# A one-layer hybrid trunk with routed experts: LayerNorm between the row sums on VectorE, the SSM and convolution tails on GpSimd in whole buffers, another table order on ScalarE, another order of work ahead of the first expert

## The chip, the cores and the metric

The kernel runs on one core of one Trainium2 chip. Its time is the device time of one execution in microseconds (us), and the figure compared is the median of several runs. The text uses the profile's names for the engines: PE is TensorE, DVE is VectorE, ACT is ScalarE, POOL is GpSimd, SP is SyncE, whose queue issues most of the DMAs. Each engine runs its own list of instructions in order and waits on semaphores for the others.

## The reference

The input is x, 1024 tokens by 1024 features, float32, one layer. Cut to what matters here:

```python
h = rms_norm(x, mix_norm)
c_q, c_kv, k_pe, u_ssm, conv_a, conv_g = split(h @ w_in)
y_attn = mla_mixer(...)     # 8 heads; q, k RMS-normed per head, rotary on 32 of 96 dims, block-causal softmax
y_ssm  = s5_mixer(...)      # z = gelu(y); out = z * sigmoid(z @ w_glu)        width 256
y_conv = conv_mixer(...)    # silu(layer_norm(conv31(a * sigmoid(g)) + b))     width 256
x = x + concat(rms_norm(y_attn), rms_norm(y_ssm), rms_norm(y_conv)) * out_norm @ w_out
h = rms_norm(x, ffn_norm)
# router: first the best of 4 groups, then the best 2 of its 8 experts, with gates
x = x + sum(gate_e * (silu(h @ w1[e]) * (h @ w3[e])) @ w2[e])   # 32 experts, d_ff 512, float32
```

## The kernel before

**Stages.** The 1024 tokens are 8 tiles of 128 (NT = 8). After the input projection, the convolution (on DVE, to 182 us) and the SSM scan, the kernel projects q, k and v tile by tile (`save_qkv` on ACT). Then come three things that this change touches: a stretch in which LayerNorm, the q/k norms and the SSM tail are made (about 206 to 262 us), the attention loop (262 to 459 us), and the stretch from the last output tile to the first expert (576 to 640 us). Behind it a loop over 34 blocks of 128 rows (32 experts and two overflow blocks) runs to the end at 1262 us.

**Norms and LayerNorm.** POOL squares the q and k of tile i (`square_qk`, L593) into two buffers that alternate, so it may be at most two tiles ahead of DVE, which sums them (`sum_qk`, L1360). POOL squares tiles 0 and 1, then waits for DVE's statistics (`ln_stats`), makes 1/sqrt of the variance (L606 and L607, `ln_rstd`), and squares tiles 2 to 7. DVE sums tiles 0 and 1, makes LayerNorm's statistics (L1371, L1374), waits for `ln_rstd`, normalizes (L1379), applies weight and bias in two operations over the whole buffer `ctok` (L1383, L1384), then sums tiles 2 to 7 (L1391). The sum of squares of all heads goes to ACT for its square root (L870), and DVE refines it. Then DVE makes head 0's q and k (`make_heads_part`, L353) and signals `head0_made`. POOL makes heads 1 to 7, and starts head 1 on `qk_scaled` (L611), which comes ahead of DVE's head 0. Two heads' buffers alternate.

**ACT's order there:** Silu of `ctok` (L854), Gelu of the SSM output in two halves (L862, signal `z_ready`), the square root (L870), the copy of the transposed z (`zT`, L873), Sigmoid (L878) behind PE's 32 matmuls with w_glu (L1894), the two copies of head 0's k (`save_kT`, L935). A change of function needs an ACT_TABLE_LOAD.

**Attention loop.** A step n is one head and one tile of queries; STEPS is 64, 8 steps a head, with the tiles in the order 7, 6, 1, 0, 5, 4, 3, 2. PE makes the scores two steps ahead, DVE takes the row maximum (L1440), ACT the exponentials (L945), PE transposes them (L1964), ACT and DVE copy them out, PE multiplies by the values once in two steps (L1976). Beside it the next head's q and k are transposed in four parts through one PSUM bank (`turn_head`, steps 1 to 4 of each head, L1912), and in heads 0 to 3 ACT does one piece of the y tail at the end of each step (`y_step`, L899):

```python
CONV_SQUARE_AT, SSM_SQUARE_AT, CONV_SCALE_AT, SSM_SCALE_AT = (range(NT * h, NT * (h + 1)) for h in range(4))
Y_TURN_AT = {NT * (3 + k // 4) + 5 + k % 4: k for k in range(NT)}
```

A square is an ACTIVATE with an accumulator, a scale another ACTIVATE (L883, L888). The product of Sigmoid and z is one DVE operation at step 3 (`gate_ssm`, L1415). POOL makes both 1/rms behind head 4 (L626 to L630). In heads 3 and 4 PE transposes y (`turn_y`) and ACT copies it. The loads of w_out wait for the last copy (L426). In heads 6 and 7 ACT and DVE split w_out and y in two parts (`high_y_piece`, `rest_y_piece`).

**Into the experts.** In the second output projection the SP queue stores each tile of h2 (the normed rows, which experts gather from) and of x2 (into `out`). Ahead of the last tile's two stores it issues three loads of 2 MB, w1 of expert 0 and w1 and w3 of expert 1 (L447 to L454); w3 of expert 0 was loaded long before. ACT waits for all stores of x2 (`out_stored`, L1049), since the rounded copy of w3 lies where x2 was, and only then makes the rounded copies of w1 and w3 (`high_w13`), four operations. POOL waits for the h2 stores and the routing table (L650, L651), copies an index for the scatter (`prepare`) and gathers expert 0's and 1's rows (L653). DVE makes the rests of w1, of the gathered rows, and of w3 (L1675 to L1677), then the overflow table (L1679 to L1704), whose signal `ov_table` lets SP issue the loads of w2 of experts 0 and 1 (L461 to L466). From then on SP issues each load when PE has used up the buffer: `next_up`, `next_down`.

Of the kernel before, what the change touches and what calls it, by code (L numbers as in the profile page):

```python
# [22 lines left out]
P = 128  # L23
# [13 lines left out]
def build(nc, x, positions, mix_norm, w_in, q_a_norm, w_uq, kv_a_norm, w_ukv, q_norm, k_norm,  # L37
# [34 lines left out]
    with ExitStack() as ctx:  # L72
# [69 lines left out]
        sout = at(S0 + 12640, NT, SW)  # L142
        cperm = at(S0 + 14592, 2, NT, P)
# [133 lines left out]
        ln_done, z_ready, glu_done, mid_squared = sems("ln_done z_ready glu_done mid_squared")  # L277
# [27 lines left out]
        conv_done, qk_mean, qk_root, qk_scaled, head0_made, heads_made, y_half_filled = sems("conv_done qk_mean qk_root qk_scaled head0_made heads_made y_half_filled")  # L305
# [33 lines left out]
        CONV_SQUARE_AT, SSM_SQUARE_AT, CONV_SCALE_AT, SSM_SCALE_AT = (range(NT * h, NT * (h + 1)) for h in range(4))  # L339
        Y_TURN_AT = {NT * (3 + k // 4) + 5 + k % 4: k for k in range(NT)}  # L340
# [33 lines left out]
        def _(sp):  # L374
# [148 lines left out]
        def _(pool):  # L523
# [78 lines left out]
            for i in range(2):  # L602
# [5 lines left out]
            for i in range(2, NT):  # L608
                square_qk(i)

            pool.wait_ge(qk_scaled, 1)  # L611
# [7 lines left out]
            for h in range(1, H):  # L619
# [108 lines left out]
        def _(act):  # L728
# [136 lines left out]
            link(last)  # L865
            act.sem_inc(z_ready, 1)
            act.sem_inc(hi_drained, 1)

            act.wait_ge(qk_mean, 1)
            act.activation(at(14336 + 2816, 2 * NT * H), qks.rearrange("p a i h -> p (a i h)"), ACT.Sqrt).then_inc(qk_root, 1)  # L870
# [1334 lines left out]
```

## Time and profile before

| | |
|---|---|
| Median of 3 runs | 1266.5 us (1263.73 to 1268.53) |
| The profiled execution | 1263.85 us, span 1262.1 us |
| PE busy | 1131.8 us (90%) |
| DVE busy | 980.6 us (78%) |
| ACT busy | 712.6 us (56%) |
| POOL busy | 376.2 us (30%) |
| DMA | 260.93 MB, mean 207 GB/s |
| Mean granted PE clock | 0.963 of full |

The span runs from the first to the last instruction of the profiled execution; 1.75 us of its time lie outside. Busy shares are averages over stages with different limits, so what counts is which wait ends last in a stretch.

### The profile page before, as it was taken

The page shows a single profiled execution, that of the slowest core. Times are in us where ns is not written, and L with a number is a line of the kernel's source. Part 1 is how long each engine was busy: PE and PEld are TensorE (multiplying, and loading weights), DVE is VectorE, ACT ScalarE, POOL GpSimd, SP SyncE. Part 2 cuts the span into 40 slices and gives each one's busy share as a digit, 9 for nine tenths or more (in the row PEclk, how much of TensorE's full clock was granted, in tenths as well). Part 3 has the DMA queues.
Part 4 walks back from the last instruction along what each step waited for, and adds up shares of the span by engine and source line. Part 5 has one row for each costly group of instructions (what it writes and reads, how often), then busy time and mean ns, then how long its engine had stood idle before and what let it go on. Part 6 is the DMA issues. An engine that isn't in the chain of part 4 may idle for free.

```text
span 1262.1 us, 15972 instructions
## 1 busy us (share of the span) xinstructions
PE 1131.8 (90%) x5636; PEld 866.9 (69%) x5636; DVE 980.6 (78%) x1179; ACT 712.6 (56%) x865; POOL 376.2 (30%) x354
## 2 busy tenths in 40 slices
PE   5899999769899889996699999999999999999992
PEld 3447565546566568785578888888877877787781
DVE  1969998865555746366699999998988998898871
ACT  5521226455555652221577777777777777777751
POOL 2304005565534000011223233333333333334221
PEclk9899989899999999997799999999999999999996
DMA  6600000000004010337399999999999999999940
GB/s 202 163 0 1 0 12 16 2 0 2 1 1 194 41 34 1 122 128 274 115 425 384 368 396 379 394 397 376 388 372 373 372 354 373 369 350 372 359 149 10
DMA packets 55484, 260.93 MB, mean 207 GB/s; under 512 B 31088, under 2 KB 31760, under 8 KB 41616
## 3 DMA queue, kind: packets, MB, share of 16 engines
q1 hardware_dynamic: 45344, 243.03, 49.8%
q0 software_dynamic: 10096, 17.34, 5.7%
q8 instruction: 26, 0.43, 0.1%
q14 instruction: 18, 0.15, 0.0%
HBM read 252.25 MB, written 26.35 MB: 221 GB/s over the span
## 4 chain that ended last, share of the span: by engine, by line
PE 56%; DVE 19%; DMA 12%; issue 4%; ACT 3%; SPq 2%; POOL 2%; DVEq 0%; POOLq 0%; ACTq 0%
PE psum L2116 25%; DMA w<-in_w 10%; PE psum L2136 10%; PE psum L2028 7%; DVE arena L1312 5%; DVE arena L1114 4%; PE psum L1976 3%; PE psum L1946 2%; PE psum L1762 2%; PE psum L1964 2%; DMA out<-arena 2%; PE psum L2106 1%; DVE am L1440 1%; PE psum L2122 1%; PE psum L1932 1%
## 5 line engine op out<-in xcount | busy, mean ns | idle before, releaser
L1652 DVE TENSOR_TENSOR w_rest<-w,w_high 128x2048 fp32r<-128x2048 f32 x136 | 305.1, 2285 | 20.2 <-ACT w_high L1036 19.7
L1036 ACT ACTIVATE w_high<-w 128x2048 fp32r<-128x2048 f32 x136 | 256.4, 1912 | 93.7 <-DMA w<-in_w 62.6
L2116 PE MATMUL psum<-w_high,xgT_high 128*128 128x512 f32 x544 | 217.8, 400 | 15.2 <-DVE xgT_rest L1645 15.1
L2116 PE MATMUL psum<-w_rest,xgT_high 128*128 128x512 f32 x544 | 213.5, 393 | 0.0
L2116 PE MATMUL psum<-w_high,xgT_rest 128*128 128x512 f32 x544 | 213.4, 392 | 0.0
L1659 DVE TENSOR_TENSOR w_rest<-w,w_high 128x2048 fp32r<-128x2048 f32 x68 | 152.4, 2282 | 1.8 <-ACT w_high L1046 1.8
L1046 ACT ACTIVATE w_high<-w 128x2048 fp32r<-128x2048 f32 x68 | 126.4, 1908 | 26.2 <-DMA w<-in_w 26.2
L2116 PEld LDWEIGHTS psum<-w_high,xgT_high 128*128 128x128 f32 x544 | 102.9, 189 | 41.3 <-issue 16.8
L671 POOL DMA_INDIRECT out<-arena,idx x34 | 91.6, 2694 | 107.5 <-DVE arena L1672 102.2
L2116 PEld LDWEIGHTS psum<-w_rest,xgT_high 128*128 128x128 f32 x544 | 103.0, 189 | 22.0
L2116 PEld LDWEIGHTS psum<-w_high,xgT_rest 128*128 128x128 f32 x544 | 103.1, 190 | 20.1
L2136 PE MATMUL psum<-w_high,heT_high 128*128 128x512 f32 x272 | 109.5, 402 | 7.3 <-DVE heT_rest L1640 7.3
L2136 PE MATMUL psum<-w_high,heT_rest 128*128 128x512 f32 x272 | 106.6, 392 | 0.0
L2136 PE MATMUL psum<-w_rest,heT_high 128*128 128x512 f32 x272 | 106.4, 391 | 0.0
L1762 PE MATMUL psum<-arena 128*128 128x512 f32 x224 | 99.5, 606 | 3.0 <-ACT arena L743 3.0
L655 POOL COPY idx<-arena 128x2 int32 (+1 forms) x34 | 36.3, 1068 | 178.0 <-PE psum L2106 163.2
L538 POOL TENSOR_SCALAR st<-st 128x1 f32<-128x1 f32 (+1 forms) x21 | 7.1, 338 | 275.9 <-ACTq L996 96.8
L664 POOL COPY idx<-arena 128x2 int32 (+1 forms) x35 | 40.4, 1156 | 143.0 <-DMA out<-arena,idx 112.2
L1762 PEld LDWEIGHTS psum<-arena 128*128 128x128 f32 x224 | 43.4, 195 | 57.4 <-issue 57.4
L945 ACT ACTIVATE arena<-psum,am 128x1024 f32<-128x1024 f32 (+3 forms) x64 | 47.4, 741 | 58.6 <-DVE am L1440 55.8
L1946 PE MATMUL psum<-arena 96*128 96x512 f32 (+1 forms) x192 | 73.6, 493 | 0.8 <-DVE arena L1431 0.8
L1312 DVE SCALAR_TENSOR_TENSOR arena<-arena,dwc 128x1024 f32<-128x1024 f32 x58 | 69.4, 1272 | 0.0
(268 smaller groups left out, 2034.9 us busy)
## 6 DMA issues: line engine op xcount, KB each, us to landing
w<-in_w SPq DMA_DIRECT2D x102, 2048.0 KB, 19.5
arena<-in_x SPq DMA_DIRECT2D x5, 1024.0 KB, 4.9
h_scratch<-arena SPq DMA_DIRECT2D x8, 512.0 KB, 2.6
out<-arena SPq DMA_DIRECT2D x8, 512.0 KB, 3.6
arena<-in_x SPq DMA_DIRECT2D x1, 3072.0 KB, 20.6
arena<-in_w_in SPq DMA_DIRECT2D x1, 2688.0 KB, 14.8
arena<-in_w_in SPq DMA_DIRECT2D x1, 2048.0 KB, 12.1
wout_y_raw<-in_w_out SPq DMA_DIRECT2D x1, 2048.0 KB, 9.2
```

Source lines behind the costliest of these rows:

```text
L671: pool.indirect_dma_start(out=out_d, out_offset=bass.IndirectOffsetOnAxis(ap=idx[:, 2 + b, 0:1], axis=0), in_=ye[b], in_offset=None, bound ...
L1036: act.activation(w13h[k][:, c, :], w13[b][k][:, c, :], ACT.Copy).then_inc(W13H_READY[k], 1)
L1046: act.activation(w2h[:, c, :], w2s[b][:, c, :], ACT.Copy).then_inc(w2h_ready, 1)
L1114: link(dve.tensor_tensor(out_, a, b_, op))
L1312: ins = dve.scalar_tensor_tensor(cacc[:, m, :], src, dwc[:, m, k:k + 1], cacc[:, m, :], M_, A_)
L1652: dve.tensor_tensor(w13l[b][k][:, c, :], w13[b][k][:, c, :], w13h[k][:, c, :].bitcast(F32), S_).then_inc(W13_SPLIT[k], 1)
L1659: dve.tensor_tensor(w2l[b][:, c, :], w2s[b][:, c, :], w2h[:, c, :].bitcast(F32), S_).then_inc(w2_split, 1)
L1762: last = pe.matmul(bank, win[:, c, c0:c0 + P], hT[:, c, 4 * half:4 * half + 4, :].rearrange("p i j -> p (i j)"), start=(c == 0), stop=(c = ...
L1946: last = pe.matmul(psum[:, 2 * (n % 2) + k, 0:w], qT[h % 2][0:QH, i * P:(i + 1) * P], kT[h % 2][0:QH, 512 * k:512 * k + w], start=True, st ...
L2028: last = pe.matmul(psum[:, 2 * (i % 2) + k, :], x_[:, c, i * P:(i + 1) * P], w_[:, c, 512 * k:512 * (k + 1)], start=(c == 0 and n == 0), s ...
L2116: last = pe.matmul(psum[:, k, :], x_[:, c, :], w_[:, c, :], start=(c == 0 and n == 0), stop=(c == KC - 1 and n == 2))
L2136: last = pe.matmul(psum[:, 5 + k, :], h_[:, c, :], w_[:, c, 512 * k:512 * (k + 1)], start=(c == 0 and n == 0), stop=(c == FC - 1 and n == 2))
```

## The change

It has five parts. (1) POOL squares four tiles ahead of `ln_rstd`, and DVE sums tiles 2 and 3 while POOL makes `ln_rstd`, 4 and 5 behind the normalization, 6 between LayerNorm's two operations and 7 behind them. POOL's head 1 waits for `head0_made`. (2) ACT takes the square root between the two Gelu halves, and Silu of `ctok` behind them. (3) The y tail leaves ACT: POOL squares and scales `ctok` and `sout` and makes the product in operations over the whole 128 x 2048 buffer; DVE sums the squares in four operations at steps 7, 9, 25 and 27. (4) The transposes of the next head move to steps 2 to 5, those of y one step later. (5) Ahead of the first expert, the last x2 and h2 tiles are stored behind one weight load and ahead of the other two; ACT rounds w1 before it waits for `out_stored`; DVE makes half of w1's rest ahead of the table and w3's ahead of the rows'; POOL gathers before it copies the scatter's index.

```diff
+        y_squares = at(S0 + 18784, NT, SW)
...
+        Y_SUM_AT = {NT - 1: 0, NT + 1: 1, 3 * NT + 1: 2, 3 * NT + 3: 3}
+        Y_TURN_AT = {NT * (3 + k // 4) + 6 + k % 4: k for k in range(NT)}
         def next_part(n):
-            return (n // NT + 1, n % NT - 1) if n // NT + 1 < H and 1 <= n % NT <= 4 else None
+            return (n // NT + 1, n % NT - 2) if n // NT + 1 < H and 2 <= n % NT <= 5 else None
...
                 if i == NT - 1:
                     sp.wait_ge(out_filled, NT)
                     sp.dma_start(w13[0][0], w1_e[0]).then_inc(W13_IN[0][0], 16)
-                    sp.dma_start(w13[1][0], w1_e[1]).then_inc(W13_IN[1][0], 16)
-                    sp.dma_start(w13[1][1], w3_e[1]).then_inc(W13_IN[1][1], 16)
+                    sp.wait_ge(x2_ready, NT)
+                    sp.dma_start(out_s[:, i, :], x2[:, i, :]).then_inc(out_stored, 16)
                 sp.wait_ge(h2_ready, i + 1)
                 sp.dma_start(h2_s[:, i, :], h2[i % 2]).then_inc(H2_OUT[i % 2], 16)
-                sp.dma_start(out_s[:, i, :], x2[:, i, :]).then_inc(out_stored, 16)
+                if i < NT - 1:
+                    sp.dma_start(out_s[:, i, :], x2[:, i, :]).then_inc(out_stored, 16)
+            sp.dma_start(w13[1][0], w1_e[1]).then_inc(W13_IN[1][0], 16)
+            sp.dma_start(w13[1][1], w3_e[1]).then_inc(W13_IN[1][1], 16)
...
-            for i in range(2):
+            for i in range(4):
                 square_qk(i)
             pool.wait_ge(ln_stats, 1)
...
+            def square_y(src):
+                pool.tensor_tensor(y_squares, src, src, ALU.mult).then_inc(mid_squared, 1)
+            def scale_y(src, col, second):
+                pool.wait_ge(mid_summed, 2 * second + 2)
+                rms(col, col + 8, CW, NT, EPS, mid_rms)
+                pool.wait_ge(mid_rms, second + 1)
+                pool.tensor_tensor(src, src, st[:, col + 8:col + 8 + NT].unsqueeze(2).to_broadcast([P, NT, CW]),
+                                   ALU.mult).then_inc(mid_scaled, 1)
-            pool.wait_ge(qk_scaled, 1)
+            pool.wait_ge(head0_made, 1)
...
-                if h == 4:
-                    pool.wait_ge(mid_squared, 1)
-                    rms(64, 72, CW, NT, EPS, mid_rms)
-                    pool.wait_ge(mid_squared, 2)
-                    rms(48, 56, SW, NT, EPS, mid_rms)
+                if h == 1:
+                    pool.wait_ge(conv_act_done, 1)
+                    square_y(ctok)
+                if h == 2:
+                    scale_y(ctok, 64, 0)
+                if h == 3:
+                    pool.wait_ge(hi_drained, R_GLU + 1)
+                    link(pool.tensor_tensor(sout, sout, yssm, ALU.mult))
+                    square_y(sout)
+                if h == 5:
+                    scale_y(sout, 48, 1)
...
-            prepare(0, 0)
             gather(0, 0)
             gather(1, 1)
+            prepare(0, 0)
...
-            act.wait_ge(ln_done, 1)
-            link(act.activation(ctok, ctok, ACT.Silu))
...
+            save_z(0)
+            act.wait_ge(qk_mean, 1)
+            act.activation(at(14336 + 2816, 2 * NT * H), qks.rearrange("p a i h -> p (a i h)"), ACT.Sqrt).then_inc(qk_root, 1)
+            link(save_z(1))
             act.sem_inc(z_ready, 1)
             act.sem_inc(hi_drained, 1)
+            act.wait_ge(ln_done, 1)
+            act.activation(ctok, ctok, ACT.Silu).then_inc(conv_act_done, 1)
             act.wait_ge(hi_filled, R_Z + 1)
...
-                y_step(n)
+                if n in Y_TURN_AT:
+                    save_y_turned(Y_TURN_AT[n])
...
-            act.wait_ge(out_stored, 16 * NT)
             act.wait_ge(out_filled, NT)
             act.sem_inc(y_saved_a, 1)
-            for k in range(2):
-                for h in range(2):
-                    high_w13(k, 0, 0, h, W13_IN[0][k], 16)
+            for h in range(2):
+                high_w13(0, 0, 0, h, W13_IN[0][0], 16)
+            act.wait_ge(out_stored, 16 * NT)
+            for h in range(2):
+                high_w13(1, 0, 0, h, W13_IN[0][1], 16)
...
             dve.sem_inc(ln_stats, 1)
+            for i in range(2, 4):
+                sum_qk(i)
             dve.wait_ge(ln_rstd, 1)
             for i in range(NT):
                 last = dve.tensor_scalar(ctok[:, i, :], pc[i], bns[:, i, 6:7], st[:, 112 + i:113 + i], S_, M_)
             link(last)
             dve.sem_inc(hi_drained, 1)
+            for i in range(4, 6):
+                sum_qk(i)
...
             tt(ctok, ctok, lnwb[:, 0, :].unsqueeze(1).to_broadcast([P, NT, CW]), M_)
+            sum_qk(6)
             tt(ctok, ctok, lnwb[:, 1, :].unsqueeze(1).to_broadcast([P, NT, CW]), A_)
             dve.sem_inc(ln_done, 1)
+            sum_qk(7)
...
-                tt(sout, sout, yssm, M_)
+            def sum_y(k):
+                col, i0 = (64, 48)[k // 2], 4 * (k % 2)
+                dve.wait_ge(mid_squared, k // 2 + 1)
+                dve.reduce_sum(st[:, col + i0:col + i0 + 4], y_squares[:, i0:i0 + 4, :], AX).then_inc(mid_summed, 1)
...
+            rest_w13(0, 0, 0, (0,))
             dve.wait_ge(tab_filled, 2)
             save_table(0, NE, 1)
             dve.sem_inc(tab_ready, 1)
...
             dve.sem_inc(y_saved_v, 1)
-            rest_w13(0, 0, 0)
+            rest_w13(0, 0, 0, (1,))
+            rest_w13(1, 0, 0)
             rest_xgT(0)
-            rest_w13(1, 0, 0)
```

## Rows read from the trace of the kernel before

**Rows 1.** Stretches, heads 0 to 5: length, busy PE, PEld, DVE, ACT, POOL; clock, DMA, GB/s.

```profile
270.91:371.03 100.12, 86.61 (x626) 60.02 (x628) 57.03 (x169) 59.56 (x156) 53.08 (x61) 0.97 0.00 1
371.03:394.92 23.89, 22.23 (x170) 15.79 (x172) 13.69 (x42) 13.00 (x31) 13.13 (x18) 1.00 0.00 1
394.92:416.38 21.46, 20.20 (x155) 13.97 (x155) 13.54 (x42) 10.64 (x25) 1.23 (x4) 1.00 0.86 343
```

**Rows 2.** The timeline of DVE from 206 us: start, us; idle before, and what ended it.

```profile
216.05 3.71 DVE L1379 TENSOR_SCALAR arena<-psum,bns,st 128x256 f32<-128x256 f32 x8 [2.11 <-POOL st L607]
...
219.91 5.44 DVE L1114 TENSOR_TENSOR arena<-arena,lnwb 128x2048 f32<-128x2048 f32 x2
...
231.03 0.95 DVE L1362 TENSOR_REDUCE qks<-arena 128x8 f32<-128x768 f32 x1 [0.88 <-POOL arena L600]
...
278.18 2.28 DVE L1114 TENSOR_TENSOR arena<-arena 128x2048 f32<-128x2048 f32 x1
```

**Rows 3.** The timeline of ACT, the same stretch.

```profile
226.70 1.91 ACT L854 ACTIVATE arena<-arena 128x2048 f32<-128x2048 f32 x1
...
229.93 1.47 ACT L862 ACTIVATE arena<-psum 128x128 f32<-128x128 f32 x8
...
233.68 1.28 ACT L870 ACT_TABLE_LOAD   x1 [0.17 <-ACT arena L862]
...
240.81 0.31 ACT L870 ACTIVATE arena<-qks 128x128 f32<-128x128 f32 x1 [5.84 <-DVEq L1398]
...
252.52 2.06 ACT L878 ACTIVATE arena<-psum 128x512 f32<-128x512 f32 x4 [8.16 <-PE psum L1894]
...
259.27 0.59 ACT L935 ACTIVATE arena<-psum 96x512 f32<-96x512 f32 x1 [4.68 <-PE psum L1932]
```

**Rows 4.** The timeline of PE, the same stretch.

```profile
243.12 9.37 PE L1894 MATMUL psum<-arena 128*128 128x256 f32 x32 [7.41 <-ACT arena L873]
...
258.14 3.44 PE L1932 MATMUL psum<-ident,arena 128*96 128x128 f32 x16 [5.66 <-DVEq L1411]
...
262.37 3.49 PE L1946 MATMUL psum<-arena 96*128 96x512 f32 x8 [0.78 <-DVE arena L1431]
```

**Rows 5.** The timeline of POOL, from 206 us.

```profile
230.95 1.47 POOL L599 TENSOR_TENSOR arena<-arena 128x768 f32<-128x768 f32 x1
...
243.58 2.21 POOL L361 TENSOR_TENSOR arena<-arena,qks 128x768 f32<-128x768 f32 x1 [5.31 <-DVEq L1407]
...
319.36 1.65 POOL L540 TENSOR_TENSOR st<-st,minus_half 128x8 f32<-128x8 f32 x1
```

**Rows 6.** The waits of head 1 (296.81 to 322.17): us in total, times, longest.

```profile
ACT arena L888 <- POOL st L540: 2.5, 1, 2.5
```

**Rows 7.** The chain of waits ahead of the first expert, its longest piece.

```profile
583.73 19.28 DMA out<-arena
```

**Rows 8.** The timeline of all engines ahead of the first expert.

```profile
598.99 0.19 DVE L1117 TENSOR_SCALAR arena<-psum 128x32 int32<-128x32 f32 x1 [3.14 <-PE psum L2073]
...
601.94 0.19 POOL L664 COPY idx<-arena 128x2 int32<-128x2 int32 x1 [20.45 <-DMA h_scratch<-arena]
...
603.14 7.31 ACT L1036 ACTIVATE w_high<-w 128x2048 fp32r<-128x2048 f32 x4 [16.05 <-DMA out<-arena]
...
606.70 1.94 PE L2106 MATMUL psum<-ident,arena 128*128 128x128 f32 x8 [7.83 <-DMA arena<-h_scratch,idx]
...
612.54 4.48 DVE L1652 TENSOR_TENSOR w_rest<-w,w_high 128x2048 fp32r<-128x2048 f32 x2
...
612.67 0.80 PE L2116 MATMUL psum<-w_high,xgT_high 128*128 128x512 f32 x1 [4.03 <-DVE xgT_rest L1645]
```

**Rows 9.** The timeline of the SP queue: the first load after the gap.

```profile
623.66 0.34 SPq L465 DMA_DIRECT2D w<-in_w  x1
```

**Rows 10.** DMA issues, windows 650:700, then 900:950: count, KB, us to landing.

```profile
w<-in_w SPq DMA_DIRECT2D x9, 2048.0 KB, 11.1
...
w<-in_w SPq DMA_DIRECT2D x9, 2048.0 KB, 21.4
```

More of the change, by code:

```diff
@@ L607, in _ @@
             pool.tensor_tensor(st[:, 112:112 + NT], st[:, 112:112 + NT], minus_half[:, 0:NT], ALU.pow).then_inc(ln_rstd, 1)
-            for i in range(2, NT):
+            for i in range(4, NT):
                 square_qk(i)
-            pool.wait_ge(qk_scaled, 1)
+            def square_y(src):
[7 more added lines that the diff above has]
+            pool.wait_ge(head0_made, 1)
             n = [0]
@@ L864, in _ @@
                                               ACT.Gelu_apprx_tanh)
-            link(last)
+                return last
+            save_z(0)
+            act.wait_ge(qk_mean, 1)
+            act.activation(at(14336 + 2816, 2 * NT * H), qks.rearrange("p a i h -> p (a i h)"), ACT.Sqrt).then_inc(qk_root, 1)
+            link(save_z(1))
             act.sem_inc(z_ready, 1)
             act.sem_inc(hi_drained, 1)
-            act.wait_ge(qk_mean, 1)
-            act.activation(at(14336 + 2816, 2 * NT * H), qks.rearrange("p a i h -> p (a i h)"), ACT.Sqrt).then_inc(qk_root, 1)
+            act.wait_ge(ln_done, 1)
+            act.activation(ctok, ctok, ACT.Silu).then_inc(conv_act_done, 1)
             act.wait_ge(hi_filled, R_Z + 1)
@@ L880, in _ @@
             act.sem_inc(hi_drained, 1)
-            def square_y(src, i, col):
-                link(act.activation(tmp[:, 0:CW], src[:, i, :], ACT.Square, accum_out=st[:, col + i:col + 1 + i]))
-                if i == NT - 1:
-                    act.sem_inc(mid_squared, 1)
-            def scale_y(src, i, col):
-                link(act.activation(src[:, i, :], src[:, i, :], ACT.Copy, scale=st[:, col + i:col + 1 + i]))
-                if i == NT - 1:
-                    act.sem_inc(mid_scaled, 1)
             def save_y_turned(k):
@@ L1364, in sum_qk @@
                 dve.sem_inc(qk_summed, 1)
-            sum_qk(0)
-            sum_qk(1)
+            kp2 = at(14336 + 2560, NT, RD)
+            for i in range(2):
+                sum_qk(i)
             dve.wait_ge(hi_filled, R_CONV + 1)
@@ L1381, in _ @@
             dve.sem_inc(hi_drained, 1)
+            for i in range(4, 6):
+                sum_qk(i)
+            dve.wait_ge(scratch_in, 16)
+            tt(kp2, kpe, kpe, M_)
+            link(dve.reduce_sum(st[:, 120:120 + NT], kp2, AX))
             dve.wait_ge(row_par_in, 16 * 8)
+            ts(qkw[:, 0, :], qkw[:, 0, :], SCALE, None, M_)
             tt(ctok, ctok, lnwb[:, 0, :].unsqueeze(1).to_broadcast([P, NT, CW]), M_)
+            sum_qk(6)
             tt(ctok, ctok, lnwb[:, 1, :].unsqueeze(1).to_broadcast([P, NT, CW]), A_)
             dve.sem_inc(ln_done, 1)
-            dve.wait_ge(scratch_in, 16)
-            kp2 = at(14336 + 2560, NT, RD)
-            tt(kp2, kpe, kpe, M_)
-            link(dve.reduce_sum(st[:, 120:120 + NT], kp2, AX))
-            ts(qkw[:, 0, :], qkw[:, 0, :], SCALE, None, M_)
-            for i in range(2, NT):
-                sum_qk(i)
+            sum_qk(7)
             tt(qks[:, 1], qks[:, 1], st[:, 120:120 + NT].unsqueeze(2).to_broadcast([P, NT, H]), A_)
@@ L1405, in _ @@
             tt(qk_f, qk_f, qkr, M_)
-            dve.sem_inc(qk_scaled, 1)
             for a in range(2):
@@ L1481, in _ @@
                         save_qT(h, part // 2)
+                if n in Y_SUM_AT:
+                    sum_y(Y_SUM_AT[n])
                 if n % 2 == 1:
                     save_ohT(n // 2)
-                if n == 3:
-                    gate_ssm()
                 if n - 1 in Y_PIECE_AT:
@@ L1601, in _, with rest_w13 @@
             ts(tokf[:, :], toki[:, :], -SKIP_ROW, None, A_)
+            def rest_w13(k, b, e, halves=(0, 1)):
+                for h in halves:
+                    c = slice(h * KC // 2, (h + 1) * KC // 2)
+                    dve.wait_ge(W13H_READY[k], 2 * e + (h + 1))
+                    dve.tensor_tensor(w13l[b][k][:, c, :], w13[b][k][:, c, :], w13h[k][:, c, :].bitcast(F32),
+                                      S_).then_inc(W13_SPLIT[k], 1)
             def normalize(i):
@@ L1646, in rest_xgT @@
                                   xgTh.rearrange("p c n -> p (c n)").bitcast(F32), S_).then_inc(xgT_saved, 1)
-            def rest_w13(k, b, e):
-                for h in range(2):
-                    c = slice(h * KC // 2, (h + 1) * KC // 2)
-                    dve.wait_ge(W13H_READY[k], 2 * e + (h + 1))
-                    dve.tensor_tensor(w13l[b][k][:, c, :], w13[b][k][:, c, :], w13h[k][:, c, :].bitcast(F32),
-                                      S_).then_inc(W13_SPLIT[k], 1)
             def rest_w2(b, e):
```

29 lines of the change are left out of this document (3 added, 26 removed).

## The prediction

> **What bounds the kernel now.** The stretches first [rows 1]. In heads 0 to 5 of the attention loop PE is busy 87% to 94% of every stretch and DVE at most 63%, but the lengths differ though PE's and DVE's work hardly do: heads 0 to 3 take 100.12 us together, 25.0 each, head 4 takes 23.89, head 5 takes 21.46. ACT goes with them, 59.6 us busy in the four, 14.9 a head, and 10.64 in head 5, which has none of the y tail. The steps are chains that go PE, DVE, ACT, PE; a piece of ACT work between two links lengthens them. Then the timelines of the four engines from 206 to 262 us [rows 2 to 5]: DVE bounds it, with its waits for POOL (2.11 us, later 0.88) and its waits for nobody; PE starts the first scores at 262.37. Then the waits of head 1 [rows 6]: ACT sat 2.5 us for POOL's 1/rms, because POOL makes it behind head 4. Last the stretch ahead of the experts: the chain of waits has a piece of 19.28 us that is one store [rows 7], since it queues behind 6 MB of weights; behind it ACT starts its roundings at 603.14, POOL its gather, PE its first expert matmul at 612.67 [rows 8]. The SP queue issues the next load at 623.66 [rows 9]. In the expert loop the weights' time to landing grows from 11.1 to 21.4 us [rows 10] while PE uses them at a steady pace: the stream is the slower of the two, and its start counts as much as PE's.
>
> **Part 1 and 2, LayerNorm and ACT's order.** DVE's idle for `ln_rstd` (2.11 us) is filled with two sums that it needs anyway, and so are four waits for POOL's squares (0.88 in the row; three more like it of 0.75, so 3.1): POOL is now two tiles ahead each time. That is 5.2 us. Against it, one of LayerNorm's two multiplies now starts beside POOL's last square. Before, the two took 5.44 us with POOL running for the first 0.96 us, against 2.28 for one alone [rows 2]: that overlap cost 0.9. Now about 2 us overlap, so I charge 0.9 to 1.4 more, and take 1.2. ACT's root, at 240.81 before [rows 3], comes at 236.8, 4.0 earlier.
>
> The SBUF page of the Trainium skill (SBUF — State Buffer, Who interferes with whom) says that a DVE operation with two SBUF inputs and a POOL operation that reads SBUF exclude each other for whole instructions. By that rule the charge would be the rest of one POOL square, 0.4 us, and the sum 0.8 better; the 0.9 us above for an overlap of 0.96 agrees with it.
>
> From the root on the new chain is ACT's. Root 0.31, table load 1.28, second Gelu half 1.47, hand-over 0.2; PE turns z under the next table load (1.28) and Silu (1.91); then the four copies of zT, priced as the Sigmoid's four of the same size, 2.06 [rows 3]. That is 8.5 us: PE's w_glu matmuls start at 245.3 instead of 243.12, and take 9.37 again [rows 4], to 254.7. Then Sigmoid 2.06 with 0.2 to hand over, and two copies of k of 0.59 each: first scores at 258.2 instead of 262.37, **4.1 us** earlier. Head 0 is not on this path any more. DVE came from the root at 240.81 to head 0's end at 258.1, where PE's turn starts [rows 4]: 17.3 us, with POOL's head 1 beside it from 243.58 on [rows 5]. Even unchanged these end at 254.1, ahead of 254.7; DVE's 2048 columns in 2.28 us give about 7 us for head 0 without POOL beside it, an end near 247. POOL's head 1, put behind it, takes some 13 us, to 260 or at the worst 267, and is first needed in step 2 of head 0, about 268. **Bounds:** if PE's matmuls run wholly at the high clock they are 2 us shorter; if the squares do not keep up, 2 of the 4.1 go.
>
> **Part 3, the y tail.** Off ACT go 8 operations per head in heads 0 to 3, off DVE the product of 2.28 us in head 0 [rows 2], which sat in the chain. On DVE come four sums of 1024 columns; 768 take 0.95 [rows 2], so 1.3 each. Those at steps 9 and 25 lie in DVE's wait for PE's longest multiply; those at 7 and 27 cost between 0 and 1.3, I take 0.7. So head 0 becomes 21.46 + 0.9 = 22.3, head 1 with half of the one at the border 21.8, head 2 21.5 (its 2.5 us wait for POOL [rows 6] gone with the rest), head 3, which has the four turns of y as head 4 has, 23.89 + 0.5 = 24.4: 90.0 instead of 100.12 [rows 1]. With 0.5 us in the first steps this is **10.6 us**. The bounds are 5 (the heads keep 23, since some other link takes the place) and 14.
>
> POOL gets, behind heads 1, 2, 3 and 5, five operations over 2048 columns. 768 columns take it 1.47 [rows 5], so 3.9 at most, and two 1/rms of 1.65 + 0.2. Beside them it needs some 13 a head (13.13 in head 4 [rows 1]), so it has room; the tight place is `turn_head(3, 0)`, step 18. The second sum comes in step 9, about 291.5; 1/rms 1.9, scale 3.9, head 3 13.1: 310.4. PE wants it at about 315, 2.1 heads behind the first scores. Slack 4.6 us.
>
> **Part 4, the later turns.** It costs nothing of itself; the parts move from the step with the longest value multiply to short ones. I take 0, between -3 and +3 over seven heads. The turns of y end a step later, so w_out's 4 MB start some 2.7 us later against step 49: at the 343 GB/s of the row of head 5 [rows 1] they need 12.3 us of the 21.5 that remain. Hidden.
>
> **Part 5, into the first expert.** The last stores queue behind 2 MB and no more: at 6 MB in about 19 us, they land some 12 us earlier, about 590. POOL's wait (601.94 before) ends with the routing table instead (DVE starts to write it at 598.99, so 599.5), and the index copy comes first: it gains 2.4, and gives back about 1.0, since DVE's rests now run beside its two copies and its gather (an operation of 768 columns takes POOL 2.21 beside DVE and 1.47 alone [rows 5]); the bounds of that are 0 and all 2.4. So rows land about 1.4 earlier, at 605.3 instead of 606.7. Then turn 1.94, ACT's copy 1.0 at once (ACT's 7.31 us of roundings [rows 8] ran to 610.46 before and now end by 596), the rest 1.24: PE starts at 609.7 instead of 612.67, **3.0 us** earlier. DVE made w3's rest (4.48 us) behind the rows' before [rows 8]; now ahead. So the overflow table starts 7 us earlier, and with it the loads at 623.66 [rows 9]. That load stream is then 4 us further ahead of PE; by the growing landing times [rows 10] PE gets nearly all of it back later as stalls that do not come. I take **6.5 us** for the end, between 3.0 (PE's own start) and 7.5.
>
> **The sum.** 4.1 + 10.6 + 6.5 = 21.2 us. Against the profiled execution's 1263.85 this is 1242.65. The median of the runs shown lies 2.65 above it, so the forecast is **1245.3 us**.
>
> **Rivals.** (a) *The heads are bound by another link.* For it: PE is busy 87% in heads 0 to 3, and in head 5 POOL was nearly idle (1.23 us), so 21.46 may be a price without POOL. Against: DVE's busy time is the same in both kinds of head. The loop would give 5 or less, 1251. Chance 0.13. (b) *The stream is paced by PE after all*, the early loads only fill buffers sooner: the end gives 3.0, and if the gather loses all to DVE 1, 1249 to 1251. For it: landing in 11.1 us still leaves PE unstalled. Chance 0.10. (c) *POOL comes late, and it ends slower.* POOL runs in order, and head 3 sits behind a sum, 1/rms and a scale, head 4 behind a product and a square. Under DVE's two-input work POOL's operations can take twice as long. At double price, 7.9 us each, head 3 comes within its slack and head 4 about 3 us late: 1248. It needs 13 us per operation to eat the 21 us; at 15.7, head 3 is 7 late and head 4 19 late, 1271. Nothing in the loop has DVE read twice from SBUF, so chance 0.02. The GPSIMD page of the Trainium skill (GPSIMD Engine Reference, Elementwise — side-by-side cycle accounting) gives 4.5 us for such an operation and would leave elementwise work on DVE; by that price the slack at head 3 is 4.0 instead of 4.6, and the sum the same. (d) *The parts cancel*, as the ACT chain of part 2 loses what part 1 gains and the heads give little: 1260 to 1266. Chance 0.03.
>
> **How the numbers follow.** The forecast has 0.72. Its own bounds, 2 us on either side in part 1, 5 and 14 for the loop, 3 and 7.5 for the end, do not all fall together: 1239 to 1251. Taking in (a) and (b) needs 1254 at the top. 0.5%, about what a measurement of this kernel can tell from no change, is 6.3 us: faster than 1260.2 holds the forecast, (a) and (b), 0.95; I leave 0.93, within 0.04, slower 0.03.
>
> **What would show it.** Right: ACT's Sigmoid starts near 254.7 and the first scores near 258; no ACT square or scale in the loop, heads 0 to 2 each under 22.5 us; POOL's head 3 done before PE asks for it; the last x2 store lands near 590, PE's first expert matmul some 3 us closer to the last output tile, SP's next load some 7 us closer. Wrong: a wait of PE for POOL in heads 2 or 3, heads above 23 us with ACT idle, or an expert loop as long as before from PE's first matmul to the end.

## The result, and the profile after

The changed kernel takes **1254.6 us** (median of five executions; 1253.5 to 1258.1) where the one before takes 1266.5 (also five): ratio 0.992, interval 0.990 to 0.994. A second measurement of the same file gave 1256.1 against 1266.0, ratio 0.991 (0.989 to 0.993). The gain is 10 to 12 us, about half of the 21.2 forecast. The profiled execution took 1256.61 us, its span 1254.5.

The stretches of heads 0 to 3, head 4 and head 5 after, with the columns of [rows 1]:

```profile
267.06:362.83 95.77, 83.66 (x624) 57.81 (x625) 60.05 (x173) 45.87 (x109) 72.40 (x71) 1.00 0.00 1
362.83:388.20 25.37, 22.27 (x170) 15.79 (x169) 13.87 (x42) 13.06 (x32) 12.58 (x15) 1.00 0.00 1
388.20:411.20 23.00, 20.41 (x154) 14.01 (x153) 13.69 (x42) 11.28 (x27) 2.88 (x9) 1.00 0.80 320
```

Heads 0 to 3 take 4.35 us less than in [rows 1], where 10.1 was forecast, and heads 4 and 5, in which the y tail never had a square or scale, are 1.5 us each **longer** though PE and DVE are busy within 0.25 us of what they were. Something new stands in every head. The waits of head 5 name it (engine and line, who is waited for, us in total, times, longest):

```profile
ACT arena L936 <- DVE am L1435: 6.9, 4, 2.7
...
PE psum L1928 <- ACT arena L926: 1.8, 2, 1.1
```

L1928 is PE's transpose of the next head's q and k (`turn_head`), L926 is ACT's copy of the turned k (`save_kT`), L936 the exponentials and L1435 DVE's row maximum. In head 5 before, PE had no wait for that copy. The timeline of all engines, after, shows the first of the two:

```profile
392.00 0.60 PE L1928 MATMUL psum<-ident,arena 128*96 128x128 f32 x4
...
392.39 0.96 DVE L1435 TENSOR_REDUCE am<-psum 128x1 f32<-128x768 f32 x1
...
392.55 1.25 PE L1942 MATMUL psum<-arena 96*128 96x512 f32 x4
...
393.38 0.90 ACT L936 ACTIVATE arena<-psum,am 128x768 f32<-128x768 f32 x1 [2.44 <-DVE am L1435]
...
394.27 0.58 ACT L926 ACTIVATE arena<-psum 96x512 f32<-96x512 f32 x1
...
394.91 0.64 PE L1928 MATMUL psum<-ident,arena 128*96 128x128 f32 x4 [1.12 <-ACT arena L926]
```

The four transposes of part 0 end at 392.60. ACT could copy them at once, but its list has the exponentials of step n+2 first, and it sits 2.44 us waiting for their row maximum. So the copy runs at 394.27, and PE, which has one bank for these turns, starts part 1 at 394.91, 1.12 us after it was ready. Part 3 loses 0.64 in the same way.

Ahead of the loop, in the timelines that answer to [rows 2] to [rows 5]:

```profile
225.30 0.98 DVE L1107 TENSOR_TENSOR arena<-arena 128x256 f32<-128x256 f32 x1
...
225.96 1.65 POOL L603 TENSOR_TENSOR arena<-arena 128x768 f32<-128x768 f32 x1
...
226.77 0.90 DVE L1110 TENSOR_SCALAR qkw<-qkw 128x96 f32<-128x96 f32 x1
227.57 1.03 POOL L604 TENSOR_TENSOR arena<-arena 128x512 f32<-128x512 f32 x1
227.71 3.05 DVE L1107 TENSOR_TENSOR arena<-arena,lnwb 128x2048 f32<-128x2048 f32 x1
...
237.57 0.31 ACT L887 ACTIVATE arena<-qks 128x128 f32<-128x128 f32 x1 [5.16 <-DVEq L1394]
...
240.91 3.60 PE L1846 MATMUL psum<-ident,arena 128*128 128x128 f32 x16 [8.69 <-ACTq L890]
...
244.55 2.06 ACT L895 ACTIVATE arena<-psum 128x512 f32<-128x512 f32 x4 [0.52 <-PE psum L1846]
...
246.67 8.86 PE L1890 MATMUL psum<-arena 128*128 128x256 f32 x32 [2.15 <-ACT arena L895]
...
255.57 2.06 ACT L900 ACTIVATE arena<-psum 128x512 f32<-128x512 f32 x4 [7.65 <-PE psum L1890]
...
258.98 3.46 PE L1942 MATMUL psum<-arena 96*128 96x512 f32 x8 [1.70 <-ACT arena L926]
```

The first scores start at 258.98 instead of 262.37. Ahead of the first expert, in the timeline of all engines, and the two rows of DMA issues (windows 650:700 and 900:950) are:

```profile
595.39 0.19 DVE L1110 TENSOR_SCALAR arena<-psum 128x32 int32<-128x32 f32 x1 [0.73 <-PE psum L2069]
...
597.19 2.25 POOL L678 DMA_INDIRECT arena<-h_scratch,idx  x1 [0.96 <-POOL idx L675]
...
603.76 1.02 ACT L1000 ACTIVATE xgT_high<-psum 128x1024 fp32r<-128x1024 f32 x1 [9.76 <-PE psum L2102]
...
606.10 0.29 PEld L2112 LDWEIGHTS psum<-w_high,xgT_high 128*128 128x128 f32 x1 [2.77 <-DVE xgT_rest L1648]
...
612.69 0.34 SPq L469 DMA_DIRECT2D w<-in_w  x1
```

```profile
w<-in_w SPq DMA_DIRECT2D x9, 2048.0 KB, 8.7
...
w<-in_w SPq DMA_DIRECT2D x8, 2048.0 KB, 20.3
```

POOL now gathers 1.8 us behind the table, and has waited for no store. ACT's four roundings ran from 586.69 to 594.00 without a pause, so the last store of x2 had landed by 590.4, as forecast. From the table's first write to PE's first expert matmul it is 10.71 us (595.39 to 606.10) instead of 13.68 (598.99 to 612.67). The next load comes 6.59 us behind that matmul instead of 10.99. But from PE's first expert matmul to the end it takes 648.4 us where it took 649.4.

### The profile page after: what moved, and what is told of

It is laid out like the page before. It is cut to its first block, busy times and chain, and to the rows that moved or that the text cites. A ratio compares the mean times of both kernels' runs of the same rounds, so it can differ in the third digit from the quotient of the medians.

```text
span 1254.5 us, 15926 instructions
## 1 busy us (share of the span) xinstructions
PE 1130.0 (90%) x5636; PEld 866.9 (69%) x5636; DVE 978.3 (78%) x1182; ACT 700.2 (56%) x818; POOL 378.5 (30%) x359
## 4 chain that ended last, share of the span: by engine, by line
PE 60%; DVE 19%; DMA 9%; issue 4%; ACT 4%; SPq 2%; POOL 0%; DVEq 0%; ACTq 0%; POOLq 0%
PE psum L2112 26%; PE psum L2132 11%; DMA w<-in_w 9%; PE psum L2024 6%; DVE arena L1305 6%; DVE arena L1107 5%; PE psum L1972 3%; PE psum L1942 2%; PE psum L1758 2%; PE psum L1960 2%; PE psum L2102 2%; DVE am L1435 1%; PE psum L2118 1%; PE psum L1928 1%; DVE arena L1110 1%
## 5 line engine op out<-in xcount | busy, mean ns | idle before, releaser
L1038 ACT ACTIVATE w_high<-w 128x2048 fp32r<-128x2048 f32 x68 | 126.3, 1908 | 20.3 <-DMA w<-in_w 20.2
L675 POOL COPY idx<-arena 128x2 int32 (+1 forms) x34 | 27.5, 808 | 201.7 <-PE psum L2102 169.0
L936 ACT ACTIVATE arena<-psum,am 128x1024 f32<-128x1024 f32 (+3 forms) x64 | 47.3, 740 | 59.7 <-DVE am L1435 58.5
L684 POOL COPY idx<-arena 128x2 int32 (+1 forms) x35 | 33.2, 948 | 113.3 <-DMA out<-arena,idx 102.8
```

The lines of the kernel that those rows point to most:

```text
L1038: act.activation(w2h[:, c, :], w2s[b][:, c, :], ACT.Copy).then_inc(w2h_ready, 1)
```

## The experiments

Two theories stood after this. **T**: the later turns cost some 1.5 us a head through ACT's copy, and the rest of the forecast is about right. Its rival **S**: the heads are long for another reason, POOL's whole-buffer work above all, and the turns are innocent. For the experts, **A**: the lead of the weight stream counts, **B**: only PE's own start does. Each ratio is against the kernel before, measured beside it (medians 1265.8 to 1266.2).

**1. The changed kernel again.**

> The changed kernel itself, on the chip of the three runs beside it. Both theories: about 10 to 12 us below the kernel before (ratio 0.991 to 0.993), heads 0 to 5 of the attention loop at 23.5, 23.0, 23.0, 26.4, 25.4 and 22.9 us, as its first trace has them.

Measured: 1256.1 us, ratio 0.991 (0.989 to 0.993); first scores at 258.71, heads 23.55, 22.98, 22.98, 26.27, 25.37, 23.00. The result repeats.

**2. The turns back.**

```diff
-Y_TURN_AT = {NT * (3 + k // 4) + 6 + k % 4: k for k in range(NT)}
+Y_TURN_AT = {NT * (3 + k // 4) + 5 + k % 4: k for k in range(NT)}
-    return (n // NT + 1, n % NT - 2) if n // NT + 1 < H and 2 <= n % NT <= 5 else None
+    return (n // NT + 1, n % NT - 1) if n // NT + 1 < H and 1 <= n % NT <= 4 else None
```

> The changed kernel with the transposes of the next head back in steps 1 to 4 and those of y back by one step; all else of the change stays. Theory T (the later turns cost 1.5 us a head, because PE, one step later, waits for ACT's copies of k, which stand behind the exponentials): heads 0 to 2 and 5 fall to 21.5 or 22, PE's waits for L926 vanish from them, first expert matmul 9 to 11 us earlier than in the changed kernel, median 8 to 11 us below it, about 1245. Rival S (the heads are longer for another reason: POOL's whole-buffer operations, DVE's sums, or ACT without its y work running differently): the heads stay within 0.5 us of 23, the median within 3 us of the changed kernel.

Measured: **1244.3 us**, ratio 0.982 (0.980 to 0.984), 11.8 less than the changed kernel on the same chip, where 8 to 11 were expected. Its stretches of heads 0 to 3, 4 and 5:

```profile
267.31:356.82 89.51, 83.06 (x626) 57.78 (x625) 59.21 (x173) 45.95 (x110) 69.49 (x68) 1.00 0.00 1
356.82:380.71 23.89, 22.23 (x169) 15.79 (x169) 13.68 (x42) 12.99 (x32) 17.08 (x23) 1.00 0.00 1
380.71:402.20 21.49, 20.23 (x154) 14.00 (x153) 13.51 (x42) 10.69 (x26) 1.25 (x4) 1.00 0.85 343
```

Heads 4 and 5 are back at the 23.89 and 21.46 of [rows 1], with the whole y tail on POOL. The turns carry all of what was missing: over heads 0 to 6 this trace is 11.3 us shorter than that of the changed kernel.

**3. The turns late, alone**, in the kernel before: the reverse of the edit of 2.

> The kernel before with nothing but the turns moved to steps 2 to 5 (and those of y one step later). Theory T: PE waits 1 to 2 us a head for ACT's copies of k, more in heads 0 to 3 where ACT still has the y tail; the head with nothing beside it (head 5) goes from 21.46 to 22.9, the median 7 to 12 us above the kernel before. Rival S: within 3 us of the kernel before, head 5 at 21.5.

Measured: 1279.7 us, ratio 1.010 (1.008 to 1.012), 13.8 slower, more than the 7 to 12 expected; head 5 is 23.01. The cost needs nothing else of the change. PE's waits in the heads before the y tail is through (270.95 to 373) are:

```profile
PE psum L1932 <- ACT arena L935: 8.6, 8, 2.2
```

Here too PE's turn (L1932 in this file) waits for ACT's copy of k (L935), eight times in four heads. In head 5, which has no y tail beside it, two such waits take 1.8 us, as in the changed kernel.

**4. The copy first.** The turns stay late; ACT's list changes.

```diff
-                if n + 2 < STEPS:
-                    exponentials(n + 2)
                 if next_part(n):
                     h, part = next_part(n)
                     if part % 2 == 0:
                         save_kT(h, part // 2)
+                if n + 2 < STEPS:
+                    exponentials(n + 2)
```

> The changed kernel with ACT's copy of k put ahead of the exponentials of the same step instead of behind them; turns stay in steps 2 to 5. Theory T with this mechanism: the copy fits into the 2.4 us that ACT waits there for DVE's maximum, PE's waits of 1.1 and 0.6 us for it vanish, heads 0 to 2 and 5 at 21.5 to 22, median 6 to 10 us below the changed kernel. If only the place of the transposes on PE costs (its own work in the short steps) and not ACT's copy, the heads stay at 23 and the median within 3 us of the changed kernel. A loss is possible where the copy delays the exponentials: then ACT's waits for DVE shrink and PE's for the exponentials grow.

Measured: **1243.3 us**, ratio 0.983 (0.981 to 0.985), 12.8 below the changed kernel where 6 to 10 were expected. Its stretches of heads 0 to 3, 4 and 5, then the same place of head 5 in the timeline:

```profile
265.91:354.43 88.52, 82.69 (x625) 58.02 (x625) 59.28 (x173) 45.96 (x109) 68.97 (x67) 1.00 0.00 1
354.43:377.93 23.50, 22.08 (x170) 15.84 (x169) 13.67 (x42) 13.07 (x32) 16.10 (x19) 1.00 0.00 1
377.93:399.07 21.14, 20.23 (x154) 14.06 (x153) 13.49 (x42) 11.31 (x27) 2.92 (x9) 1.00 0.87 348
```

```profile
381.73 0.60 PE L1928 MATMUL psum<-ident,arena 128*96 128x128 f32 x4
...
382.12 0.96 DVE L1435 TENSOR_REDUCE am<-psum 128x1 f32<-128x768 f32 x1
...
382.37 0.59 ACT L926 ACTIVATE arena<-psum 96x512 f32<-96x512 f32 x1 [1.69 <-PE psum L1928]
383.12 0.90 ACT L936 ACTIVATE arena<-psum,am 128x768 f32<-128x768 f32 x1 [0.15 <-DVE am L1435]
383.36 0.60 PE L1928 MATMUL psum<-ident,arena 128*96 128x128 f32 x4
```

The copy fits into what was ACT's wait, the exponentials start 0.04 us behind the row maximum, and PE's second turn comes 1.63 us behind the first instead of 2.91. One swap of two calls takes the cost away with the turns where they were, so the late copy is the cause. The heads are even 0.35 us shorter than with the turns back (21.14 against 21.49).

**5. Both**, turns back and copy first.

> The changed kernel with the turns at steps 1 to 4 as before and ACT's copy of k ahead of the next exponentials. Theory: the cost is ACT's copy standing behind exponentials that wait for DVE's row maximum; with the copy first the place of the turns does not matter, so heads are 21.0 to 21.7 us and the median lies within 2 us of the copy-first version (1243.3). Rival: the place of the turns has a price of its own (they lengthen PE's longest step), then it is 2 to 5 us slower or faster than copy-first.

Measured: 1246.2 us, ratio 0.984 (0.982 to 0.986); heads 0 to 3 take 89.50 and head 5 21.49, as in 2. With the turns at steps 1 to 4 the place of the copy does not matter, since PE had no such wait there. The theory's second half, that with the copy first the place of the turns does not matter either, missed its 2 us: the later place is the better one, by 1.7 us over heads 0 to 5 in the two traces. The medians lie 2.9 apart, but were taken on two chips, and the intervals of their ratios overlap; so the size of this smaller effect is not settled.

**6. Parts 1 and 2 alone** (LayerNorm between the sums, ACT's order, POOL's head 1 behind head 0), on the kernel before.

```diff
             save_z(0)
+            act.wait_ge(qk_mean, 1)
+            act.activation(at(14336 + 2816, 2 * NT * H), qks.rearrange("p a i h -> p (a i h)"), ACT.Sqrt).then_inc(qk_root, 1)
             link(save_z(1))
...
-            pool.wait_ge(qk_scaled, 1)
+            pool.wait_ge(head0_made, 1)
```

> The kernel before with parts 1 and 2 alone: LayerNorm between the sums, POOL four tiles ahead, root between the Gelu halves, Silu behind them, POOL's head 1 behind head 0; the y tail, turns and part 5 as before. First scores at 258.5 to 259.5 instead of 262.4, heads as before. If these 3.4 us are kept to the end: 3 to 4 us faster, about 1262.5. Rival: POOL's head 1, made behind head 0, is late for the turns at step 1 of head 0, and head 0 grows by 1 to 3 us; then 0 to 2 us faster.

Measured: 1261.2 us, ratio 0.997 (0.995 to 0.999), 5.0 faster, where 3 to 4 were expected; first scores at 258.13. Head 0 takes 24.30 us, as it does in the trace of part 5 alone (24.29), which changes nothing ahead of it. The rival falls.

**7. Part 3 alone** (the y tail on POOL, DVE's four sums), on the kernel before.

```diff
+                if h == 1:
+                    pool.wait_ge(conv_act_done, 1)
+                    square_y(ctok)
...
-                y_step(n)
+                if n in Y_TURN_AT:
+                    save_y_turned(Y_TURN_AT[n])
```

> The kernel before with part 3 alone: the y tail on POOL in whole buffers, DVE's four sums, turns at steps 1 to 4 as before. The prediction's part 3: heads 0 to 2 under 22.5 us, head 3 at 24.4 to 24.6, heads 4 to 7 as before, 10.6 us faster in all. By difference from the other runs (21.7 with the turns back, less 5.0 for the norms and 5.5 for part 5) it should be 10 to 12 us faster than before, 1254 to 1256. Rival: another link binds the heads and the gain is 5 us, 1261.

Measured: 1256.2 us, ratio 0.993 (0.990 to 0.995), 9.6 faster. Heads 0 to 3 in its trace:

```profile
272.78:362.28 89.50, 83.06 (x626) 57.75 (x625) 59.23 (x173) 46.02 (x110) 62.69 (x60) 1.00 0.00 1
```

That is 10.6 us less than in [rows 1], with ACT 13.5 us less busy. But the execution of [rows 1] is not a clean base. Its granted clock in the four heads is 0.97, because it was 0.93 in heads 0 and 2. The same unchanged heads in the trace of part 5 alone:

```profile
271.79:368.79 97.00, 83.52 (x625) 57.70 (x625) 57.05 (x169) 59.45 (x156) 52.97 (x61) 1.00 0.00 1
```

So 3.1 of the 10.6 us are clock, and at a clock of 1.00 on both sides part 3 is worth 7.5 in these heads. Of the four traces with unchanged heads, three have one or two heads at 0.93 or 0.94; of the eight with part 3 none has. Whether that is a part of the gain or chance stays open. The median says 9.6, with an interval of 6 to 12.

**8. Part 5 alone**, and **9. part 5 without DVE's order**, on the kernel before. The second lacks

```diff
+            rest_w13(0, 0, 0, (0,))
             dve.wait_ge(tab_filled, 2)
...
-            rest_w13(0, 0, 0)
-            rest_xgT(0)
-            rest_w13(1, 0, 0)
+            rest_w13(0, 0, 0, (1,))
+            rest_w13(1, 0, 0)
+            rest_xgT(0)
```

> The kernel before with part 5 alone (store order, ACT's and POOL's order, DVE's rests). In the whole change PE's first expert matmul came 4.9 us closer to the output projection's start and SP's next load 7.7 us closer, yet from the first expert to the end only 1.0 us of the stream's lead came back, and the clock fell in the last blocks. Theory A, the lead of the weight stream counts as the prediction had it: 5.5 to 7.5 us faster than before, about 1259.5. Rival B, PE paces the blocks and only its own start counts: 3 to 5 us faster, about 1261.5. Heads as before (25.9 to 21.5 us), first scores at 262.4.

> Part 5 without DVE's order of the rests: stores, ACT's and POOL's order as after, DVE as before. SP's next load should come 4 to 7 us later than with all of part 5, since w3's rest (4.48 us) stands ahead of the overflow table again; PE's first expert matmul the same or up to 1 us earlier. Theory A (the stream's lead counts): 2 to 4 us slower than part 5 alone. Rival B (only PE's start counts): the same as part 5 alone within 1 us.

Measured: 1260.7 us (0.996, 0.995 to 0.997) and 1262.6 (0.997, 0.996 to 0.999): 5.5 and 3.7 faster. PE's first expert matmul stands 10.7 and 10.8 us behind the table, some 3.0 less than before; the next load is issued 6.6 us behind that matmul with DVE's order and 11.0 without. The medians lie 1.9 us apart, which is neither A's 2 to 4 nor B's 1, and their intervals overlap. In the two traces 4.4 us of the difference already stand ahead of the table, and 1.2 from PE's first expert matmul to the end. This pair does not separate A from B.

**10. w3's rest behind the rows' again**, in the copy-first kernel.

```diff
             rest_w13(0, 0, 0, (1,))
-            rest_w13(1, 0, 0)
             rest_xgT(0)
+            rest_w13(1, 0, 0)
```

> The copy-first kernel with DVE's rest of w3 (4.48 us) behind the rest of the gathered rows again: PE's first expert matmul at the same distance from the output projection (149 us), SP's next load 3 to 5 us later. Theory A, the stream's lead counts as the prediction had it: 2 to 4 us slower than copy-first (1243.3). Rival B, only PE's start counts: within 1 us of it.

Measured: 1244.7 us, ratio 0.984 (0.982 to 0.987), where copy-first has 1243.3. The medians are of two chips, but up to the experts the two traces agree: PE's first expert matmul starts at 591.93 in the copy-first kernel and at 591.94 in this one. The SP queue from there, first in the copy-first kernel, then in this one:

```profile
598.53 0.33 SPq L469 DMA_DIRECT2D w<-in_w  x1
...
599.39 0.42 SPq L476 DMA_DIRECT2D w<-in_w  x1
604.70 0.33 SPq L478 DMA_DIRECT2D w<-in_w  x1
```

```profile
602.93 0.33 SPq L469 DMA_DIRECT2D w<-in_w  x1
...
603.79 1.11 SPq L476 DMA_DIRECT2D w<-in_w  x1
604.94 0.47 SPq L478 DMA_DIRECT2D w<-in_w  x1
```

Three loads come 4.40 us earlier; the fourth waits until PE has used up a buffer and comes 0.24 earlier. PE's waits behind 900 us are then (the copy-first kernel first):

```profile
PE psum L2112 <- DVE xgT_rest L1648: 6.6, 10, 1.2
```

```profile
PE psum L2112 <- DVE xgT_rest L1648: 8.3, 10, 1.4
```

The spans differ by 0.7 us (1240.3 and 1241.0), the stalls by 1.7, the medians by 1.4. Theory A wanted 2 to 4, B under 1, and the difference of the medians is within their intervals. Nor do the stalls alone decide it: in the other traces with the early loads this wait is 5.7 to 9.1 us. All thirteen traces say more. From PE's first expert matmul to the end, the seven with the loads 6.6 us behind it take 648.2 to 651.3 us (mean 649.1), the six with 11.0 take 649.1 to 651.9 (mean 650.1). A lead of 4.4 us is worth about 1 us, if anything; the ranges overlap.

**11. The copies of y first, too**: the same rule applied to `save_y_turned`.

```diff
+                if n in Y_TURN_AT:
+                    save_y_turned(Y_TURN_AT[n])
                 if n + 2 < STEPS:
                     exponentials(n + 2)
-                if n in Y_TURN_AT:
-                    save_y_turned(Y_TURN_AT[n])
```

> The copy-first kernel with ACT's copies of the turned y also ahead of the next exponentials. Theory: any copy from that one bank that stands behind exponentials waiting for DVE's row maximum delays PE's next turn; heads 3 and 4 (24.6 and 23.5 us) each have four such turns and should lose 1 to 2 us each, about 1241. Rival: in heads 3 and 4 PE's own 32 more transposes are the length, and nothing changes (within 1 us of 1243.3).

Measured: 1244.3 us, ratio 0.983 (0.980 to 0.985). The trace shows what the theory wanted, heads 0 to 3 and head 4:

```profile
268.37:355.34 86.97, 82.33 (x625) 58.10 (x625) 59.27 (x173) 45.90 (x108) 67.79 (x65) 1.00 0.00 1
355.34:377.26 21.92, 21.69 (x168) 15.89 (x169) 13.68 (x43) 13.15 (x31) 15.93 (x19) 1.00 0.00 1
```

That is 1.55 us less in the four, all in head 3, and 1.58 less in head 4. The median does not show the gain: it is 1.0 above copy-first, on another chip, with intervals that overlap. In this execution the first scores start 2.45 us later, 1.5 us more lie between the last head's first value multiply and the output projection, where the granted clock was 0.83 for 20 us and in copy-first for 10, and 1.6 more ahead of the first expert. Whether such losses take the 3 us back as a rule, or in this execution alone, stays open.

## Why the prediction was half right

**Parts 1 and 2: right.** Forecast 4.1, measured 3.4 in the first scores of the whole change and 5.0 alone. The root came at 237.57, 3.2 us earlier and not 4.0. The charge of 1.2 us more for POOL's squares beside DVE was right as a sum (1.13), but lay elsewhere: the multiply lost 0.76, less than the 0.9 before [rows 2], and two small operations ahead of it, which had nothing beside them before and took 0.42 and 0.21, took 0.98 and 0.90. The missing 0.8 is in the short gaps between DVE's operations. The prediction took back the whole of each wait for POOL, 0.75 and 0.88, but a gap of some 0.15 stays when the wait is gone: besides those waits the gaps were 1.05 us together, and now they are 1.81. From the root on 21.4 us were forecast to the first scores, and it took 21.41, by two errors that cancel: PE turned z in 3.60 us, 1.94 in the kernel before, at a granted clock of 0.50 from 240 to 244 us (the lower level, 1.2 GHz) and after 8.69 us of idling, and so ACT waited 0.52 for it; w_glu's matmuls gave that back, 8.86 instead of 9.37. The trace of these parts alone does not keep all of it: from the first scores to head 0's first value multiply it takes 10.00 us at a clock of 0.83, where before it took 8.54 at 1.00. So the 5.0 of the medians is not explained by this trace.

**Part 3: the mechanism right, the tenth by luck.** 100.12 to 89.5 us for heads 0 to 3 [rows 1], forecast 90.0; 9.6 us in the medians, forecast 10.6. The prediction put all that heads 0 to 3 had above head 5 down to ACT's y tail, but its own row has a clock of 0.97, and 3.1 us of it were that clock (experiment 7). POOL's whole-buffer operations took 3.60 (square and scale) and 4.54 (product), forecast 3.9 at most; in the changed kernel head 3 was made at 310.0, forecast 310.4, and PE never waited for it. Rival (c) falls. Rival (a), that some other link keeps the heads at 23 us, named the number that came in the changed kernel (23.0), but not its cause: the link was made by part 4, and without it the heads are 21.5.

**Part 4: the failed step.** "It costs nothing of itself; the parts move from the step with the longest value multiply to short ones. I take 0, between -3 and +3 over seven heads." It cost 11.8 us in the changed kernel and 13.8 in the one before. The sentence priced the PE time of a moved part, and for that it was right: with the copy first the later place gains 1.7 over heads 0 to 5. What it left out is the other engine that the part needs. A turn is PE, then a copy by ACT or DVE, then the next turn through the same bank. ACT's copies are those of parts 0 and 2. Moved to even steps, they have only scores and one to five transposes behind them on PE, which is back at the bank 1.2 us later (392.60 to 393.79), while ACT stands in a wait for the row maximum. In odd steps PE has a value multiply behind the turn, and that hid a late copy. The trace before had both, in head 5: ACT's waits, and PE's turns of parts 2 and 3:

```profile
ACT arena L945 <- DVE am L1440: 8.1, 6, 2.7
```

```profile
400.65 0.64 PE L1932 MATMUL psum<-ident,arena 128*96 128x128 f32 x4 [0.20 <-DVE arena L1431]
...
403.49 0.60 PE L1932 MATMUL psum<-ident,arena 128*96 128x128 f32 x4
```

Part 2 ended at 401.29 and ACT's copy, behind its exponentials, only at 403.18, yet part 3 started at 403.49 without a wait for it: 0.3 us of room, which the value multiply and its neighbours on PE had made. So six of the eight steps have exponentials that wait for DVE, and ACT's list has the copy behind them. The move was priced on PE's list and not on ACT's. The prediction's own sign of being wrong, heads above 23 us with ACT idle, is what came: in heads 0 to 3 ACT was busy 46 of 96 us. One part of the term was right: no engine waited for the loads of w_out, which start later.

**Part 5: half right.** PE's own start: forecast 3.0, measured 2.97 behind the table. The stream: "PE gets nearly all of it back later as stalls that do not come", 3.5 of some 4. It got about 1 of 4.4, and that not clear of the spread between traces (experiment 10). The landing times did shrink early (8.7 against 11.1), but that lead is held by three loads; from the fourth on each load waits for a buffer that PE frees, and by the window 900:950 the landings stood at 20.3 against 21.4 [rows 10]. Rival (b) described this better than the forecast. Part 5 alone measured 5.5 in the medians, and its trace is 5.2 shorter than the one before: 3.0 are PE's start behind the table, 2.4 lie ahead of the table, where heads 0 and 2 had the better clock, and nothing (-0.2) was gained behind PE's start. So 3.0 is what is shown for part 5.

**The sum.** Alone, parts 1 and 2, part 3 and part 5 gave 5.0, 9.6 and 5.5. Less the 11.8 that part 4 cost inside the change that is 8.3 us (6.3 with the 13.8 that it cost alone), and the whole gave 9.9 (experiment 1). Without part 4 they add to 20.1, and the kernel with the turns back gave 21.7, at 1244.3; the forecast of 1245.3 is that kernel's. The copy-first kernel, 1243.3, is the best run, 1.7% under the kernel before and 1% under the changed one.

## What to carry to other kernels

A step that is moved is moved on every engine that serves it: look at where the copy that frees its buffer stands on that engine's list, and at what that engine waits for just ahead of it. On an engine that runs in order, a short copy for which all is ready belongs ahead of an operation that is going to wait; shown here for the copies of k, while for those of y the trace shows it and the median does not. A lead of a stream counts only as far as its buffers hold it; read it from the first load that waits for a buffer, not from the first load issued. And look at the clock column of the rows that serve as a base: a stretch that ran at 0.93 is longer for a reason that the change need not touch.

## What the runs showed of the hardware

**DVE beside POOL.** In the copy-first kernel LayerNorm's multiply and POOL's square met the other way round from the changed kernel, whose rows stand above. The timelines of DVE and POOL:

```profile
226.93 2.29 DVE L1107 TENSOR_TENSOR arena<-arena,lnwb 128x2048 f32<-128x2048 f32 x1
```

```profile
227.10 3.45 POOL L603 TENSOR_TENSOR arena<-arena 128x768 f32<-128x768 f32 x1 [1.18 <-ACTq L868]
```

Where DVE was first, it kept its 2.29 us, and POOL's square, begun 0.17 later, took 3.45: the 2.12 that DVE still ran and 1.33 more, about its 1.47 alone [rows 5]. Where POOL was first (227.57, 1.03), DVE took 3.05: the 0.89 that POOL still ran and 2.16. The small scaling of 96 columns that ran into a POOL square ended just behind it, too (227.67 and 227.61), after 0.90 us instead of 0.21. All three agree with what the SBUF page of the Trainium skill (SBUF — State Buffer, Who interferes with whom) says, that whichever of DVE and POOL is first at the ports they share keeps them for its whole instruction. The scaling has one input, which by that section contends only in a two-port mode; no row shows which mode it ran in. The prediction's rule of thumb, 0.9 us for 0.96 of overlap, fits where POOL was first (0.76 lost for 0.89) and not where DVE was: there DVE lost nothing and POOL lost 1.98.

**The price of a POOL operation over 2048 columns.** 3.60 us where both inputs are one buffer or one is broadcast, 4.54 for two whole buffers. The 4.5 us of the GPSIMD page of the Trainium skill (GPSIMD Engine Reference, Elementwise — side-by-side cycle accounting) is met by the second and not by the first. Its advice to leave elementwise work on DVE was not tested: part 3 took most of this work from ACT, only the product from DVE, and no run here put the rest on DVE. What is shown is that the whole move to POOL, which had room, gave 9.6 us.

**The clock decides microseconds in one chain.** The same 32 matmuls with w_glu took 8.86 us in the changed kernel and 7.17 in the copy-first one, whose code up to there is the same. In the stretch 248 to 252 us, first the changed kernel, then copy-first:

```profile
248.00:252.00 4.00, 4.00 (x13) 3.28 (x12) 0.00 (x0) 0.00 (x0) 3.77 (x4) 0.60 0.02 4
```

```profile
248.00:252.00 4.00, 4.00 (x20) 3.53 (x19) 0.00 (x0) 0.00 (x0) 3.69 (x5) 1.00 0.00 0
```

The granted clock was 0.60 in the one and 1.00, the 2.4 GHz level, in the other, in both after 2.15 us of idle PE ahead of the matmuls; the idle stretch before the transposes of z was 8.69 us in the one and 6.05 in the other. The time gained was given back at once: the eight matmuls of the first scores then took 3.46 us in the changed kernel, at a clock of 1.00, and 5.15 in copy-first, at 0.68 from 256 to 260 us. First scores came between 256.1 and 259.0 in the eight executions that have parts 1 and 2, so one trace can't confirm a forecast to a few tenths for this chain.
